# Residual rows a step ahead, and one unit's columns by way of VectorE and DRAM, in an eight-core layer

## The reference

```python
x = LN(ALPHA * x + 0.5 * (silu(x @ f1_wg) * (x @ f1_wu)) @ f1_wd)       # x1; hidden width 2816
z = x @ w_in + b_in                                                     # 2560 columns: a, gate, g_b, g_c, b
u = a * sigmoid(gate);  ua = silu(LN(dwconv31(u) + b_dw_a))
v = g_c * b;            ub = g_b * dwconv3(v)
x = LN(ALPHA * x + concat(ua, ub) @ w_o + b_o)                          # x2
x = LN(ALPHA * x + 0.5 * (silu(x @ f2_wg) * (x @ f2_wu)) @ f2_wd)       # y
```

## Time and profile before

| what | us |
|---|---|
| median of three runs | 1190.94 |
| lowest of the three | 1188.15 |
| profiled execution, its time | 1190.59 |
| profiled execution, its span on the slowest core (7) | 1189.0 |
| spans of the eight cores | 1183.3 to 1189.0 |
| mean granted TensorE clock, all cores | 0.998 to 0.999 of full speed |

### The profile page before, as it was taken

The page is one execution under the profiler, slowest core; times in us unless marked ns, Lnnn a source line. Parts: engine busy times, 40 slices in busy tenths (PEclk is TensorE's granted clock), DMA queues, the critical chain, the costliest instruction groups (busy, mean ns, idle before and its releaser), DMA issues.

```text
span 1189.0 us, 20140 instructions; the slowest of 8 cores (1183.3 to 1189.0 us)
## 1 busy us (share of the span) xinstructions
PE 1170.9 (98%) x7080; PEld 634.8 (53%) x7080; DVE 621.7 (52%) x938; ACT 222.1 (19%) x423; POOL 194.7 (16%) x310
## 2 busy tenths in 40 slices
PE   8999999999999999999999999999999999999997
PEld 4544444455555666554455555544444466666444
DVE  2213218866555564718877556563837722222366
ACT  3211110021222235320022122323200021121000
POOL 0111112311100023212111010122212210000111
PEclk9999999999999999999999999999999999999999
DMA  8899987998867679985567766669987654443033
GB/s 283 115 210 142 141 149 179 187 188 126 118 106 113 128 122 178 198 181 146 169 156 112 112 109 120 126 127 178 194 191 193 205 118 76 72 74 87 25 108 106
DMA packets 83762, 168.50 MB, mean 142 GB/s; under 512 B 9744, under 2 KB 39632, under 8 KB 82368
## 3 DMA queue, kind: packets, MB, share of 16 engines
q0 software_dynamic: 29504, 78.16, 44.7%
q1 hardware_dynamic: 54160, 89.06, 26.4%
HBM read 212.17 MB, written 33.95 MB: 207 GB/s over the span
## 4 chain that ended last, share of the span: by engine, by line
PE 87%; DMA 7%; DVE 3%; issue 1%; SPq 1%; POOL 0%; ACT 0%; DVEq 0%; POOLq 0%; ACTq 0%
PE ps L587 47%; PE ps L651 22%; PE ps L751 11%; PE ps L1034 4%; DMA sb_xr<-x1s 3%; DMA xscr<-sb_tq 2%; PE ps L869 1%; DMA sb_RW<-xta 1%; PE ps L669 1%; DMA sb_xA<-xscr 1%; DVE sb_RW L813 1%; PE ps L975 0%; PE ps L1003 0%; SPq L453 0%; PE ps L657 0%
## 5 line engine op out<-in xcount | busy, mean ns | idle before, releaser
L587 PE MATMUL ps<-sb_xB,sb_ring 128*128 128x352 bf16 (+1 forms) x2112 | 319.6, 310 | 0.0
L587 PE MATMUL ps<-sb_xA,sb_ring 128*128 128x512 bf16 (+1 forms) x1472 | 310.8, 370 | 2.5 <-ACT sb_xA L1225 1.9
L594 DVE TENSOR_TENSOR sb_hT<-sb_sg,ps 128x352 bf16<-128x352 f32 (+3 forms) x224 | 129.7, 580 | 347.9 <-PE ps L587 323.3
L651 PE MATMUL ps<-sb_RW,sb_hT 128*128 128x512 bf16 x1364 | 295.7, 379 | 0.0
L587 PEld LDWEIGHTS ps<-sb_xB,sb_ring 128*128 128x128 bf16 x2112 | 205.9, 98 | 106.9 <-issue 1.1
L592 ACT ACTIVATE sb_sg<-ps 128x352 f32<-128x352 f32 (+3 forms) x224 | 113.9, 509 | 617.2 <-PE ps L587 495.7
L587 PEld LDWEIGHTS ps<-sb_xA,sb_ring 128*128 128x128 bf16 x1472 | 143.2, 98 | 159.5 <-issue 5.2
L651 PEld LDWEIGHTS ps<-sb_RW,sb_hT 128*128 128x128 bf16 x1364 | 133.2, 98 | 160.2 <-issue 0.4
L373 POOL DMA_DIRECT2D sb_ring<-wgu x84 | 46.5, 554 | 458.4 <-PE ps L587 406.5
L484 POOL TENSOR_SCALAR sb_mv<-sb_mv 128x1 f32<-128x1 f32 (+1 forms) x50 | 44.8, 896 | 330.9 <-DVE sb_mv L482 323.9
L476 DVE SCALAR_TENSOR_TENSOR sb_xr<-sb_xr,ps 128x1024 f32<-128x1024 f32 x47 | 57.2, 1218 | 65.2 <-PE ps L651 57.6
(11 more groups left out here) (103 smaller groups left out, 598.6 us busy)
## 6 DMA issues: line engine op xcount, KB each, us to landing
sb_ring<-wgu POOLq DMA_DIRECT2D x84, 512.0 KB, 7.7
sb_RW<-wd POOLq DMA_DIRECT2D x33, 512.0 KB, 11.0
sb_wring<-win POOLq DMA_DIRECT2D x40, 256.0 KB, 5.6
sb_RW<-uscr SPq DMA_DIRECT2D x128, 67.0 KB, 5.1
sb_xr<-xp SPq DMA_DIRECT2D x16, 512.0 KB, 7.6
x1s<-sb_xr SPq DMA_DIRECT2D x16, 512.0 KB, 4.7
sb_xr<-x1s SPq DMA_DIRECT2D x16, 512.0 KB, 10.7
x2s<-sb_xr SPq DMA_DIRECT2D x16, 512.0 KB, 7.5
```

What stands on the lines that cost most here:

```text
L587: ins = e.matmul(bank(bk, n), lhsT=ring[:, s, c:c + 128], rhs=xcol(k, tok0, n), start=(k == 0), stop=(k == KC - 1))
L594: P.op("dve", lambda e: e.tensor_tensor(out=hT[:, f, l0:l0 + n], in0=sg[:, q, :n], in1=bank(bu, n), op=ALU.mult), reads=[("sg", q)] + pst( ...
L651: ins = e.matmul(ps[:n, (yb + h) * 512:(yb + h + 1) * 512], lhsT=hT[:, f, l0:l0 + n], rhs=wd[:, f, h * 512:(h + 1) * 512], start=(f == 0), ...
```

## The change

- In `unit_E`, step A0 loads the residual rows of the unit's tiles 0 and 1, and every later step A those of the tile after its own.
- `gate[0]` is emptied after the first down.
- The four `load_wo` move from the first down into steps of `block_C` in mixer 0.
- Unit 0's tiles are no longer cast and transposed by ScalarE and TensorE; unit 1's still are.
- `refill` at the end of mixer 0 loads x2 of tiles 0 to 3 from DRAM, as bf16, into the four slots of `wring`. In the following down, after the matmuls of its first position, `xmove` sends these four tiles by way of VectorE and the scratch; behind them POOL fetches the two weight chunks that the last two up items now hold back (`hold=2`), and the four `win` chunks.
- In mixer 1 the credit after step B0 of unit 2 is 1.0 instead of 0.65.

```diff
-        def up_items(which, b, hooks=None):
+        def up_items(which, b, hooks=None, hold=0):
...
-                            fetch_wgu(base + f + NSLOT)
+                            if f < NFC - hold:
+                                fetch_wgu(base + f + NSLOT)
...
-                    x1t = [("x1", q) for q in ((tl[k] // 2 * 2, tl[k] // 2 * 2 + 1) if tl[k] < 16 else (16,))]
-                    xslot[k] = load_xr(tl[k], prow(xsp[0], tl[k]), x1t)
+                for k in ((0, 1) if i == 0 else (i + 1,)):
+                    if k < nt:
+                        x1t = [("x1", q) for q in ((tl[k] // 2 * 2, tl[k] // 2 * 2 + 1) if tl[k] < 16 else (16,))]
+                        xslot[k] = load_xr(tl[k], prow(xsp[0], tl[k]), x1t)
...
                 for k in at(i, 5, True):
-                    if b == 0:
+                    if u == 1:
                         xpose(tl[k], xbs[k], ((3, 3, 3, 7), (3, 6, 3, 7))[par][k])
                 for k in at(i, 4, True):
-                    if b == 0:
+                    if u == 1:
                         xbs[k] = cast_xb(tl[k], xslot[k])
...
             for i, th in enumerate(cs[1:]):
                 side.append((th, gC))
+                if b == 0 and i in (6, 8, 10, 12):
+                    side.append((lambda i=i: load_wo(i // 2 - 3), 0.0))
...
-            side.append((ea.pop(0)[1], gC))
+            side.append((ea.pop(0)[1], 1.0))
...
                 def refill():
-                    wstate["lim"] = 40
-                    for _ in range(NWIN):
-                        fetch_win()
+                    for j in range(4):
+                        P.op("pool", lambda e, j=j: e.dma_start(out=wring[:, j, :], in_=spill(1, j)),
+                             reads=[("x2", j)], writes=[("wring", j)], dma="wring%d" % j)
...
-            aux[i + 4] = aux.get(i + 4, []) + [fetch_win, lambda i=i: load_wo(i)]
+            aux[i + 4] = aux.get(i + 4, []) + [fetch_win]
...
-        merge(up_items(0, 1), mixer(0, 0, pend, 3.0, 1.0, 1.0))
+        gate[0] = ()
+        merge(up_items(0, 1, hold=2), mixer(0, 0, pend, 3.0, 1.0, 1.0))
         load_ln(0)
-        pend = down(0, 1, 2.0 * ALPHA, 4.0 * EPS, False, npar=2)
+        def refill():
+            wstate["lim"] = 40
+            fetch_wgu(2 * NFC - 2 + NSLOT)
+            fetch_wgu(2 * NFC - 1 + NSLOT)
+            for _ in range(NWIN):
+                fetch_win()
+        aux = {0: [lambda: [xmove(j, j, wring, "wring") for j in range(4)], refill]}
+        pend = down(0, 1, 2.0 * ALPHA, 4.0 * EPS, False, npar=2, aux=aux)
```

## The result

| | before | after |
|---|---|---|
| median of the runs, us | 1190.94 | 1196.66 (five runs, 1195.74 to 1197.07) |
| profiled execution, us | 1190.59 | 1196.11 |
| its span on the slowest core, us | 1189.0 (core 7) | 1194.5 (core 3) |

The ratio of the times is 1.0063, 95% interval 1.0052 to 1.0075. It is taken from undisturbed runs only, of the kernel before 1188.15, 1188.57 and 1190.94, so it is not the quotient of the two medians. The changed kernel is slower by 0.5 to 0.8%: less than the 2% that separates a clear change from none, but the forecast of 1190.4 is missed and so is its range, by 1.7 us at the upper end.

What follows compares the result with a forecast made beforehand. TensorE, busy 98% of the span, was taken to bound the kernel. Terms: 1190.59 - 2.94 - 1.76 - 0.94 + 0.3 + 5.2 = 1190.4 us, no change; range 1184 to 1195.

Steps and rivals of the forecast that it cites:

- the new work: x2 reload, four VectorE transposes, sixteen scratch writes, four moves at the second down projection: cost 5.2 us, bounds 0 and 9.0.
- first writes landed at 537.5 + 1.0 = 538.5: Second down projection: first scratch writes land 1.0 us behind the last residual row; third transpose to 539.9, fourth to 541.0.
- The sentence on POOL's held fetches: Two held weight fetches on POOL behind the x2 loads, used only after the down projection: cost 0; same for four win loads.
- rival A: Scratch writes overtake or residual rows land earlier, VectorE is back in time in the second down projection: 1185.2; chance 0.25.
- d: VectorE's lateness at tile 0's residual add in the second down projection: 5.6 us, 541.0 instead of 535.4.
- The conversion: VectorE's lateness less 0.44 us costs TensorE 5.2 us: 3.8 at position 7 of the second down projection, 1.38 at 613.60.
- Gate and step ahead: Without the false hT reader and with earlier rows, both VectorE stalls go, closing TensorE holes of 0.63 and 2.31: gain 2.94 us.
- Unit 0's transposes: Four tiles' transposes leave TensorE, 0.44 us per tile: gain 1.76 us.
- Output weights: Moving their loads to mixer 0 closes the first hole, near 261 us: gain 0.94; cost in the projections taken as 0.3.
- It stays: The TensorE hole of 0.65 us at 763 us remains despite the larger credit in unit 2: 0.
- B: Slower: scratch writes move at the full DMA pace heading the second down projection, lateness 9.4, cost 9.0: 1194.3; chance 0.15.
- C: hT waits go but output projections wait for the next add; only transposes and moves are gained: 1193.3; chance 0.1.

Runs made afterwards that it cites:

- the experiment on the rows: Changed kernel with the second and third residual rows of the second down projection issued on SP behind the scratch writes: 1194.61 us, single execution.
- four-buffer variant: Changed kernel with the third and fourth transposition of the four writing into idle xb2, so none waits for scratch writes: 1186.12 us, ratio 0.9977.
- run with seven multiplies: four-buffer variant plus seven unused VectorE multiplies ahead of the first residual add of the second down projection: 1190.06 us, ratio 1.0014.
- run with seventeen multiplies: four-buffer variant plus seventeen unused VectorE multiplies ahead of the first residual add of the second down projection: 1197.9 us, ratio 1.0086.
- x2 part undone: Changed kernel without the x2 reload, its VectorE transpositions, moves and held fetches; all other edits stay: 1187.11 us, ratio 0.9986.
- x2 part alone: Kernel before plus only the x2 reload, four VectorE transposes, moves and held fetches: 1197.56 us, ratio 1.0076.

## Why the prediction was wrong

**The step that failed** is in the new work: "first writes landed at 537.5 + 1.0 = 538.5". All ahead of it came as forecast, some 3 us earlier as expected: x2 tiles by 531.5, the row at 534.0, the third transposition held by `tq`'s two buffers. But the writes landed 3.1 to 7.7 us behind that row, not 1.0. I had read their order from a stretch where a single store stood ahead of them, and asked only what was ahead on their own queue. In that stretch POOL's queue was silent while the writes moved: from 220.5 to 223.5 the trace of the kernel before has 472 packets of 512 B from SP's queue and none from POOL's. The sentence on POOL's held fetches, "They go to POOL behind the x2 loads and are used only after the down projection: 0", and the one on the `win` loads behind it priced them by who uses them, not by what flies beside them. With those fetches away the writes came in right behind the row; with two of the rows away they still came in behind fetches, packet for packet. The rule on turns, cited with the experiment on the rows, stands in the same section of the Trainium skill that the forecast drew on for rival A; it would have told that POOL's fetches count. So d was 11.9, not 5.6, and beyond even the upper bound of 9.4, which had again counted one queue's pace.

**The conversion held.** "Cost = d - 0.44" gives 11.5 us for d = 11.9, and the forecast's own sum with it, 1190.59 - 5.64 + 0.3 + 11.5 = 1196.8, against 1196.11 for the profiled execution. That it comes so near has luck in it: its start, 1190.59, lies 1.4 us above the mean of the runs behind the ratio, and its gains of 5.34 are about as much too high (below). The slope has no such help: from the four-buffer variant to the changed kernel d grew by 10.0 us and the time by 10.2. The places were partly others: with d = 5.6 the stall would have stood at position 7 and at 613; with 11.9 it begins at position 3, in the four holes of 9.42 us. (The run with seven multiplies had d = 5.65 on its slowest core, and there the largest hole, 2.17 us, does stand ahead of position 7.) The rest of the 11.5 is the lower clock, 30.63 us for 132 matmuls where the same count took 28.66 in the kernel before, 2.0. That is no cost on top of the lateness: TensorE still waits for VectorE at 621.95, so a faster TensorE would have waited longer. The run with seventeen multiplies bears this out: the same distance from the add to the end as on cores without a fall. Core 7 of the changed kernel is an exception: its clock falls a second time behind a hole at 584, no wait for VectorE follows, and its distance is the longest, 644.0.

**Gate and step ahead:** right as to the cause of both waits. Emptying the gate is enough, and with it empty, taking the step ahead out changes nothing that the times show. The size, 2.94 us, was one core's: the holes of the earlier trace rows stand on core 7 of one execution, the time is that of the slowest of eight, and the same two holes cost the other cores 0 to 2.57 us. Measured 1.5. The same holds for the sum of the gains: 5.34 forecast, 2.7 measured with four buffers (ratio 0.9977); that run still has d of 1.9 in it, by the conversion 1.5 us, so about 4.2.

**Unit 0's transposes:** 32 instructions fewer, as forecast; 1.76 was not measured apart. **Output weights:** the hole at 261 went, but no run ties that to the move, since it stayed away with the weights back in place. A cost showed as the forecast had it, a wait for `win`: at most 0.31 us in the changed kernel, on cores that are not its slowest, and 0.26 to 1.67 us on the slowest core of three other runs, where 0.3 was taken. **"It stays"**, of the 0.65 at 763: 0.23 in the changed kernel and in the four-buffer variant, 0.65 with the x2 part undone and the credit kept, 0.22 with the x2 part alone and the old credit. So it went with the x2 part, not the credit; by what path was not tried.

**The rivals.** B, 1194.3, had the right side and the right queue of events, but its bound on the writes was too low. A's condition, no wait for the writes, was made by hand in the four-buffer variant, and gave 1186.1 against its 1185.2. C falls: no output projection waited in place of the multiplies.

## What to carry to other kernels

When a step waits for a small transfer, list everything in flight when it is issued, on every queue, and take its landing from a stretch with the same company; order behind one store of its own queue says little. Here the number of packets set the pace, not the bytes. Where an engine has no slack for the next fifty microseconds, the lateness at its head is the cost, so the start is the number to bound widely, and two more buffers there were worth 10 us. And read holes on all cores before counting them as gains: on eight cores a hole that only the slowest one has is worth no more than its distance to the next.

## What the runs showed of the hardware

Small writes of one queue and large loads of another moved packet for packet and landed by turns, not in order of issue: with both queues busy SP's sent 146 packets of 512 B while POOL's sent 148 of 4096 B, and scratch writes issued at 521.6 and 521.9 landed 0.1 to 0.2 us behind two weight fetches, at 532.3 and 534.7. With POOL quiet 502 small packets went in one us, and four writes, issued 1.8 us apart, landed within 0.6 us.

A TensorE hole of 5.22 us was followed by a granted clock of 0.66 in the ten microseconds from 550 and about 2 us of slower matmuls, one of 2.17 us by 0.85 from 580 to 590. This cost nothing where TensorE still waited for VectorE behind it.
